# An accumulating weight transfer that waits for the read-back of the residual X, in a two-block transformer kernel

## The reference, cut to what matters

```python
def hybrid_mixer(h, w_in, ..., w_branch, w_out):
    ...                                  # three branches ya, yb, yc
    br_d = jnp.einsum("bsnc,ncd->bsnd", br, w_branch)
    g = jax.nn.sigmoid(gates.reshape(bsz, seq, N_BRANCHES, D_MODEL))
    merged = jnp.sum(g * br_d, axis=2)
    return merged @ w_out

def swiglu(h, w_gate, w_up, w_down):
    return (jax.nn.silu(h @ w_gate) * (h @ w_up)) @ w_down

def first_block(x, mem, ...):
    x = x + hybrid_mixer(rms_norm(x, ...), ...)
    x = x + memory_cross_attention(rms_norm(x, ...), mem, ...)
    x = x + swiglu(rms_norm(x, ...), ...)
    return rms_norm(x, final_g)
```

## Time and profile before

| | |
|---|---|
| median of 3 timed runs | 1653.83 us (1653.13 to 1653.97) |
| the profiled execution | 1647.99 us |
| its span | 1646.3 us |
| PE busy | 1623.7 us, 99% of the span |
| DVE busy | 1010.8 us, 61% |
| ACT busy | 731.3 us, 44% |
| POOL busy | 153.3 us, 9% |
| SP's hardware queue q1 | 197.29 MB, 34.6% of the 16 DMA engines' span |
| POOL's software queue q0 | 26.77 MB, 7.6% |
| mean granted TensorE clock | 0.997 of full |

### The profile page before, as it was taken

How to read it: one execution, slowest core, us unless ns; L and a number is a source line. 1 busy time by engine, 2 the same in 40 slices (tenths; PEclk the granted TensorE clock), 3 DMA queues, 4 the chain that set the end, 5 groups by cost and what they waited for, 6 DMA issues and landing times.

```text
span 1646.3 us, 21110 instructions
## 1 busy us (share of the span) xinstructions
PE 1623.7 (99%) x8434; PEld 1343.8 (82%) x8434; DVE 1010.8 (61%) x1460; ACT 731.3 (44%) x1105; POOL 153.3 (9%) x172
## 2 busy tenths in 40 slices
PE   9999999999799999999999999999999999999999
PEld 7788878888678878888988887877777888898889
DVE  5446754554474444655755675756655688767886
ACT  5344334333354343334433356246685455444453
POOL 0000001221210002000000042212101200000000
PEclk9999999999899999999999999999999999999999
DMA  7253222258744114769685453331213232363225
GB/s 268 90 194 106 84 91 72 95 144 259 210 140 154 65 51 148 219 205 233 192 269 177 135 171 102 99 150 60 78 39 128 77 103 96 113 201 106 95 88 180
DMA packets 60082, 225.96 MB, mean 137 GB/s; under 512 B 6656, under 2 KB 7040, under 8 KB 56336
## 3 DMA queue, kind: packets, MB, share of 16 engines
q1 hardware_dynamic: 55856, 197.29, 34.6%
q0 software_dynamic: 3840, 26.77, 7.6%
q10 hardware_dynamic: 288, 0.54, 0.1%
HBM read 220.35 MB, written 50.36 MB: 164 GB/s over the span
## 4 chain that ended last, share of the span: by engine, by line
PE 94%; DVE 2%; ACT 2%; DMA 1%; issue 1%; POOL 0%; SPq 0%; ACTq 0%; DVEq 0%; POOLq 0%
PE pst L504 92%; DMA X<-xT 1%; PE pst L1013 1%; PE pst L672 1%; DVE WL L1828 0%; ACT WH L1132 0%; ACT L1137 0%; DVE qx L2072 0%; ACT misc L1132 0%; POOL acc L2653 0%; DVE ZL L1836 0%; PE pst L794 0%; DVE ML L1836 0%; DVE misc L2607 0%; DVE XL L1840 0%
## 5 line engine op out<-in xcount | busy, mean ns | idle before, releaser
L504 PE MATMUL pst<-XH,WH 128*128 128x512 f32 x1312 | 522.7, 398 | 0.6 <-DVE WL L1828 0.6
L1828 DVE TENSOR_TENSOR WL<-raw,WH 128x1024 fp32r<-128x1024 f32 (+2 forms) x334 | 381.5, 1143 | 219.5 <-ACT WH L1132 218.8
L504 PE MATMUL pst<-XH,WL 128*128 128x512 f32 x1312 | 511.4, 390 | 0.0
L504 PE MATMUL pst<-XL,WH 128*128 128x512 f32 x1312 | 510.9, 389 | 0.0
L1132 ACT ACTIVATE WH<-raw 128x1024 fp32r<-128x1024 f32 (+3 forms) x336 | 326.3, 974 | 312.6 <-PE pst L504 307.2
L504 PEld LDWEIGHTS pst<-XH,WH 128*128 128x128 f32 x1312 | 246.3, 188 | 61.6 <-issue 11.5
L504 PEld LDWEIGHTS pst<-XL,WH 128*128 128x128 f32 x1312 | 246.5, 188 | 52.1 <-issue 2.6
L504 PEld LDWEIGHTS pst<-XH,WL 128*128 128x128 f32 x1312 | 246.2, 188 | 51.9
L504 PE MATMUL pst<-TH,WH 128*128 128x256 f32 (+1 forms) x586 | 170.5, 291 | 1.6 <-DVE X L2178 1.0
L504 PE MATMUL pst<-TL,WH 128*128 128x256 f32 (+1 forms) x586 | 170.1, 290 | 0.0
L504 PE MATMUL pst<-TH,WL 128*128 128x256 f32 (+1 forms) x586 | 170.0, 290 | 0.0
(11 more groups left out here) (286 smaller groups left out, 1906.8 us busy)
## 6 DMA issues: line engine op xcount, KB each, us to landing
raw<-wst SPq DMA_DIRECT2D x237, 512.0 KB, 3.3
sums<-wd POOLq DMA_DIRECT2D x8, 2816.0 KB, 20.0
raw<-sums SPq DMA_DIRECT2D x32, 384.0 KB, 3.2
sums<-wd SPq DMA_DIRECT2D x16, 704.0 KB, 6.1
sums<-sums SPq DMA_DIRECT2D x16, 704.0 KB, 6.0
raw<-wd SPq DMA_DIRECT2D x24, 384.0 KB, 3.4
raw<-sums SPq DMA_DIRECT2D x24, 320.0 KB, 2.9
raw<-wd SPq DMA_DIRECT2D x18, 320.0 KB, 3.1
```

The lines of the kernel that those rows point to most:

```text
L504: return nc.tensor.matmul(out, lhs, rhs, start=start, stop=stop, skip_group_check=more)
L1828: vec.tensor_tensor(WL[:, i % NHL, 0:n], raw[:, i % NRAW, 0:n], WH[:, i % NHL, 0:n].bitcast(F32), ALU.subtract).then_inc(wl, 1)
```

## The change

One wait is added on POOL, between the last addition of `branch(2)` and the accumulating transfer of the third plane: POOL waits until the last of the four read-back loads of X has landed.

```diff
             sum_in(1, 0, 3, 128)
             sum_in(1, 1, 3, 128)
             drain(branch(2))
+            pool.wait_ge(x_in[3], 32)
             sum_in(1, 2, 0, 192)
             for k in range(7):
                 add_squares()
```

## The result

The changed kernel takes 1641.03 us in the median of 4 runs (1638.41 to 1644.36), against 1653.48 us for the kernel before, also 4 runs (1652.27 to 1653.97). The ratio is 0.9927, with a 95% interval of 0.9906 to 0.9948: 8.6 to 15.5 us less. In a second comparison, of five runs against nine, the ratio was 0.9939 (0.9925 to 0.9953). The forecast was 1643.4 us, between 1637.5 and 1648.0, and a gain of 10.4 us. The profiled execution takes 1638.41 us with a span of 1636.7, against 1647.99 and 1646.3.

The account below looks back on a forecast made before the run. PE was taken to bound the kernel, busy 99% of the span, its largest stall being late X. Stall 8.53 plus clock 1.85 gave 10.4 us, so 1653.83 - 10.4 = 1643.4 us, range 1637.5 to 1648.

Parts of the forecast that it names:

- The stall: PE's wait for WL at 431.67 us vanishes because X lands at 425.5 instead of 438.2: 8.53 us gained.
- the deadline of 429.7: Latest landing of the first load of X without a PE stall; 425.5 us expected, 4.2 us on the safe side.
- The clock: Nine matmuls from 440.20 to 444.09 us run at full clock, 2.04 us instead of 3.89: 1.85 us gained.
- Nothing behind it: After 447.73 us PE, DVE and ACT move forward as a block: no further gain and no payback.
- POOL's wait: POOL passes the added wait at 429.4 us, reaches the squares by 430.3: zero price, at most about 1 us on ACT.
- The moved transfer: Accumulation runs from about 430.5 to 449 or 452 us beside weight chunks; price zero.
- 27 us of buffers: Five weight buffers at 5.45 us each cover late weight chunks beside the moved transfer.
- the account of how the queues share: From 417 to 438 us POOL's queue took 69.2% of DMA time, SP's 21.8%, with 1.77 MB moved.
- The 5.84 us between profile and timed runs: Timed runs of the kernel before lie 5.84 us above its profiled execution; difference taken over unchanged.
- The second rival: Larger gain: the 5.84 us of timed runs sit in the same stall, 16.2 us go, 1637.6 us; chance 0.06.
- the third: Slower: the moved transfer starves the weight queue, w_out chunk 6 late at 448.0 us, up to 1666 us; chance 0.03.
- the fourth: No effect: loads of X slow by themselves or POOL's wait met early; time stays 1653.8 us; chance 0.04.

Follow-up runs that it names:

- no_sum: Kernel before, without the new wait, the third plane's accumulating transfer cut to 16 of its 352 rows: ratio 0.9944, median 1640.2 us.
- fill_gap: Kernel before, with 36 useless matmuls on PE in its 8.5 us idle gap between w_out's tiles 2 and 3: ratio 0.9995.
- two_sums: Changed kernel, with a second 2816 KB accumulating transfer issued right ahead of the third plane's: 1639.75 us in its one run.
- late_sum: Kernel before, without the new wait, third plane's accumulation put behind POOL's first seven additions of squares: ratio 0.9967, median 1645.9 us.
- x_first: Kernel before, without the new wait; SP issues the four loads of X ahead of the memory tokens' load: ratio 0.9999.
- again: Changed kernel once more, no edit, five runs against nine of the kernel before: ratio 0.9939.
- fill_norm: Changed kernel, with ten useless matmuls on PE ahead of the norm's sums at about 985 us: ratio 0.9931, median 1639.76 us.
- late_small: late_sum with the third plane's accumulation in rows of 2 KB instead of 8 KB: ratio 0.9931, median 1640.6 us.
- wait_x0: Changed kernel, but POOL waits for the first of the four loads of X, not the last: ratio 0.994, median 1639.91 us.

## Why the prediction was right

**The stall.** Right, in place and size. PE's 8.53 us are gone. The first load landed after 6.1 us and let DVE start at 427.22 us, 426.1 on the clock of before, where 425.5 was expected; the deadline of 429.7 left 3.6 us. no_sum shows that the accumulation was the only cause.

**The clock.** 1.85 us were expected and the changed kernel's clock stayed at 1.00. Profile against profile, the span fell by 9.6 us. With the 0.8 us of the early wait for XL this is 10.4, the sum; with the 1.1 us by which DVE and SP are later just ahead of the read-back it is 10.7. fill_gap limits what this term means: alone, without DVE being early, it is worth nothing measurable.

**Nothing behind it.** DVE was abreast of PE at the third addition, where in the earlier trace rows it was at the fourth, and the wait of 1.6 us in the next stage kept its size. It moved as a block.

**POOL's wait.** The issue came at 431.55 us (430.5 on the clock of before) instead of 429.4. The squares behind it were not late for anyone.

**The moved transfer.** 21.4 us in the new place, in the expected range of 19.7 to 21.4, and free; two_sums shows that even twice its length is. A busy DVE did not hold it up, as the rows had said: DVE worked for 6.5 and 8.0 of 10 us beside it. The reason given, 27 us of buffers, was right for this stage but incomplete. The buffers only bridge a lack: a chunk in 5.45 us is a demand of 96 GB/s, and 4 KB rows got 74 GB/s beside 8 KB ones in late_sum. That kernel shows the same transfer starving a stage that wants 193. The prediction had no term for how far the new place lies from that stage: some 15 us in the changed kernel, none with two_sums, whose second transfer landed at about 469 us.

**The step that was weak** is the account of how the queues share. The text gave the read-back's slowness to a share of 21.8% of the time and 1.77 MB. That is a mean over two regimes, 145 GB/s for tokens and 45 for X. It did no harm to the sum, which needed only the rate without the accumulation, and it spoiled the expectation of x_first.

**The median.** 12.45 us in the first comparison and about 10 in the second, for 10.4 expected. The 5.84 us between profile and timed runs were not to be taken over unchanged: the changed kernel's median lies 2.62 us above its profile. Those 3.2 us less, and 0.8 us more in the profile than forecast, make 1641.03 out of 1643.4. How near a median of four comes is also luck, since these runs spread over 6 us with their clock. The second rival (the timed runs' 5.84 us belong to this stall) is refuted: the kernel before also ran at 1648.5 us with the stall in it, and the 5.84 us go with lower clock elsewhere, which the change doesn't touch. The starvation of the third did not happen, and the fourth is out.

## What to carry to other kernels

Before a transfer that nobody needs soon is issued, look at what is about to be issued on the other queue and who waits for it; a wait on that other transfer's semaphore is enough, and it need cover only the part wanted first. Then look at the stage into which the transfer moves: compare what the weights there demand per us with what their row length gets beside it. If it can't be moved, try shorter rows for it: the queues shared by packets here, so the length of a contiguous row decided who won. It has a price: the accumulation took 25.6 and 29.5 us in short rows, for 19.7 and 20.0 in long ones.

## What the runs showed that I had not expected

**Turns by the packet.** Nearly equal counts of packets where both queues had work: 100 and 104 with 8 KB rows on both sides, 223 and 224 with 2 KB rows of SP against 8 KB rows of POOL, 782 and 781 with 2 KB on both. Single stretches of 2 us stray further (33 of SP to 46 of POOL in late_sum). Beside 8 KB rows SP's queue had 145, 74 and 45 GB/s for rows of 8, 4 and 2 KB, where it reached 406 alone.

**The lower clock behind short stalls.** PE's wait of 2.5 us for TL, near 986 us in the kernel again and 6 to 13 us later in the slower kernels, was followed by the lower clock in eight profiles, that of the kernel again among them, and not in three: those of before, of the first changed one and of x_first. PE was busy and at 1.00 ahead of it each time. Behind the stall at 467 us it was seen after 2.7 us of idleness in fill_norm and late_sum and not in late_small, and never after 1.6 or 1.7. Near 1231 us it came behind 1.9 us in two profiles. So no length of stall seen here decides it. The changed kernel's runs with a mean clock of 1.000 and of 0.997 lie 6 us apart (1638.41 and 1644.36), half the gain of the whole change.

**A collision of DVE and POOL sets the stall at 467 us.** Just ahead of it an XL of DVE and an addition of POOL start 0.03 us apart. In the changed kernel XL takes 0.75 us and the addition 1.87; in fill_norm XL takes 1.86 and the addition 1.28. DVE's and POOL's rows, first of the changed kernel, then of fill_norm:

```profile
461.87 0.75 DVE L1840 SCALAR_TENSOR_TENSOR XL<-X,colsb,XH 128x512 fp32r<-128x512 f32 x1
461.90 1.87 POOL L2653 TENSOR_TENSOR acc<-acc,misc 128x512 f32<-128x512 f32 x1 [3.63 <-ACT misc L1132]
...
461.56 1.86 DVE L1843 SCALAR_TENSOR_TENSOR XL<-X,colsb,XH 128x512 fp32r<-128x512 f32 x1
461.59 1.28 POOL L2656 TENSOR_TENSOR acc<-acc,misc 128x512 f32<-128x512 f32 x1 [3.62 <-ACT misc L1135]
...
468.23 0.79 PE L504 MATMUL pst<-WH,MH 128*128 128x512 f32 x1 [2.70 <-DVE WL L1831]
```

The 1.1 us more on DVE are the 1.1 us by which PE's stall grows from 1.6 to 2.7. late_sum and late_small have the pair of fill_norm and a stall of 2.7 us; again, no_sum, two_sums and wait_x0 have that of the changed kernel and 1.6 to 1.7 us. DVE starts first by 0.03 to 0.04 us in all of them, so the order is not it. What decides which of the two is held up was not tried and stays open.
